# VectorE's attention order, 64x64 inverses on four array quarters, and an overwritten product ahead of each decay and rate product

## The reference, cut to what matters

```
def rwkv_step(S, inp):
    r_t, w_t, k_t, v_t, kk_t, b_t = inp
    sa = jnp.einsum('bhvk,bhk->bhv', S, -kk_t)
    S = S * w_t[:, :, None, :] + sa[..., None] * b_t[:, :, None, :] + v_t[..., None] * k_t[:, :, None, :]
    return S, jnp.einsum('bhvk,bhk->bhv', S, r_t)
```

## Time and profile before

| | us |
|---|---|
| median of 3 runs (4037.75 to 4045.4) | 4042.69 |
| the profiled execution | 4034.62 |
| its span, first to last instruction | 4032.9 |
| TensorE busy | 3566.0 |
| VectorE busy | 1768.2 |
| ScalarE busy | 1299.9 |

### The profile page before, as it was taken

One profiled execution on the slowest core, in us unless ns is written; L12 is line 12 of the kernel. 1 busy time (PEld: TensorE's weight loads), 2 busy tenths in 40 slices (PEclk: granted clock), 3 DMA queues, 4 the chain that ended last, 5 costly groups with the idle time before them and its releaser, 6 DMA issues. The chain is left out here.

```text
span 4032.9 us, 84425 instructions
## 1 busy us (share of the span) xinstructions
PE 3566.0 (88%) x32662; PEld 3292.9 (82%) x32662; DVE 1768.2 (44%) x2693; ACT 1299.9 (32%) x2505; POOL 161.6 (4%) x188
## 2 busy tenths in 40 slices
PE   6988689978888999999889985998698889999996
PEld 6988467768878999999878873777588789999996
DVE  3254445534654343333443534555345543333344
ACT  3343344414452111111333434443235521111113
POOL 0010000001000000000200000000001000000002
PEclk9999789979999999999989987989799899999998
DMA  2122220107541111111121123001176211111111
GB/s 93 53 68 68 69 62 26 68 25 262 210 140 32 42 43 50 42 48 46 46 70 51 62 70 100 21 26 73 61 256 220 95 37 47 47 42 46 47 47 54
DMA packets 240704, 298.79 MB, mean 74 GB/s; under 512 B 26616, under 2 KB 195952, under 8 KB 239504
## 3 DMA queue, kind: packets, MB, share of 16 engines
q1 hardware_dynamic: 224368, 227.83, 17.8%
q0 software_dynamic: 16032, 66.75, 4.3%
HBM read 228.91 MB, written 65.63 MB: 73 GB/s over the span
## 5 line engine op out<-in xcount | busy, mean ns | idle before, releaser
L767 PE MATMUL PS<-HH,WH 128*128 128x352 f32 (+2 forms) x3584 | 1194.4, 333 | 86.1 <-PEq L751 85.4
L767 PE MATMUL PS<-HH,WL 128*128 128x352 f32 (+2 forms) x3584 | 1167.6, 326 | 0.0
L767 PE MATMUL PS<-HL,WH 128*128 128x352 f32 (+2 forms) x3584 | 1166.4, 325 | 0.0
L767 PEld LDWEIGHTS PS<-HH,WH 128*128 128x128 f32 x3584 | 687.4, 192 | 104.8 <-issue 100.8
L767 PEld LDWEIGHTS PS<-HH,WL 128*128 128x128 f32 x3584 | 687.8, 192 | 2.8 <-issue 0.3
L767 PEld LDWEIGHTS PS<-HL,WH 128*128 128x128 f32 x3584 | 685.4, 191 | 0.0
L2307 DVE TENSOR_TENSOR WL<-WRAW,WH 128x1024 fp32r<-128x1024 f32 x192 | 243.6, 1269 | 680.2 <-DVEq L2306 680.2
L1517 ACT CAST WH<-WRAW 128x1024 fp32r<-128x1024 f32 x216 | 226.3, 1048 | 632.8 <-ACTq L1526 585.1
L1487 PE MATMUL PS<-GH,WH 128*128 128x352 f32 x1056 | 340.1, 322 | 0.0
L1487 PE MATMUL PS<-GH,WL 128*128 128x352 f32 x1056 | 339.5, 322 | 0.0
L1487 PE MATMUL PS<-GL,WH 128*128 128x352 f32 x1056 | 339.5, 322 | 0.0
(11 more groups left out here) (324 smaller groups left out, 4879.9 us busy)
## 6 DMA issues: line engine op xcount, KB each, us to landing
WRAW<-in_w_gate_up SPq DMA_DIRECT2D x88, 512.0 KB, 3.7
W<-split_dram SPq DMA_DIRECT2D x48, 512.0 KB, 4.6
WRAW<-in_w_down SPq DMA_DIRECT2D x44, 512.0 KB, 3.4
WH<-split_dram SPq DMA_DIRECT2D x40, 512.0 KB, 3.8
WL<-split_dram SPq DMA_DIRECT2D x40, 512.0 KB, 4.7
WRAW<-in_w_in SPq DMA_DIRECT2D x38, 512.0 KB, 3.8
raw_dram<-MIX SPq DMA_DIRECT2D x24, 528.0 KB, 3.1
R<-raw_dram SPq DMA_DIRECT2D x24, 512.0 KB, 4.5
```

The lines of the kernel that those rows point to most:

```text
L767: ins = e.matmul(out, lhs(k, wp), rhs(k, xp), start=first, stop=(k == n - 1 and xp == 1))
```

## The change

Four things change. In VectorE's attention `tile`, `normalised(1)` moves ahead of `rotary`, and the `lo` of the first two of the four due groups moves ahead of the masks. In the inverse, the blocks of head 1 are kept on the rows of the other chunk, so that the four blocks of a tile use all four 64x64 quarters of the array; each head has its own PSUM bank, both products of a level share one semaphore, and TensorE waits once in the middle of `level_right`. To put one operand there, `by_token` replaces one of its four transposes by a half one and two 64x64 products. Ahead of each decay or rate product of 512 columns, for the pairs after the first, a full 128-row product with the identity writes the same PSUM bank; the real product then overwrites it.

```diff
@@ constants: masks 128 wide, the attention masks in another order ...
-    C_AE = C_LV + LEVELS * 2 * CHUNK
+    C_AE = C_LV + LEVELS * 2 * P
...
+    def inverse_rows(h, c):
+        return slice((c ^ h) * CHUNK, (c ^ h) * CHUNK + CHUNK)
+    def column_of(u, x, h, part=0):
+        return (left_bank(u) + h) * 512 + part * 256 + x * CHUNK
+    def by_head(x, tiles):
+        return x[:, 0:2 * tiles, :].rearrange("p (a h y) t -> p h a (y t)", h=2, y=2)
+    def half_banks(u, part, tiles):
+        at = left_bank(u) * 512
+        return PS[:, at:at + 1024].rearrange("p (h z) -> p h z", h=2)[:, :, part * 256:part * 256 + tiles * HEAD]
@@ TensorE, by_token
-                transposes([... for o, a in enumerate((BB, KF, VV, KK))], 6 + x % 2, "chain_for_scalar", take)
+                for o, a in enumerate((BB, KF, VV)):
+                    e.matmul(PS[:, at + o * P:at + (o + 1) * P], rows_of(j, a)[:, tok:tok + P], ident, is_transpose=True, start=True, stop=True)
+                e.matmul(PS[:, at:at + HEAD], kk[0:HEAD, tok:tok + P], CST[0:HEAD, C_I64:C_I64 + HEAD], is_transpose=True, start=True, stop=True)
+                for c in range(2):
+                    ins = e.matmul(PS[inverse_rows(1, c), at + HEAD:at + P], kk[HEAD:P, tok + c * CHUNK:tok + (c + 1) * CHUNK],
+                                   CST[HEAD:P, C_I64:C_I64 + HEAD], start=True, stop=True)
@@ TensorE, level_left
-                    returned(a)
-                        ins = e.matmul(PS[r, at:at + CHUNK], masked_part(j, 0, u)[r, g, :], XX[u][r, g, :], start=True, stop=True)
+                    returned(a, b)
+                        ins = e.matmul(PS[inverse_rows(h, c), at:at + CHUNK], masked_part(j, 0, u)[r, g, :], XX[u][r, g, :], start=True, stop=True)
@@ TensorE, level_right
-                            ins = e.matmul(PS[r, at:at + CHUNK], XT[u][r, g, :], T1[u][r, g, :], start=True, stop=True)
-                        ins.then_inc(S("chain_for_vector"), 1)
-                        ins = e.matmul(PS[r, at:at + CHUNK], T1[u][r, g, :], XT[u][r, g, :], start=True, stop=True)
+                            e.matmul(PS[r, at:at + CHUNK], XT[u][i, g, :], T1[u][i, g, :], start=True, stop=True)
+                    for head in range(2):
+                        for x, h, g, c, r, p in blocks(tiles):
+                            if h == head:
+                                ins = e.matmul(PS[i, at:at + CHUNK], T1[u][i, g, :], XT[u][i, g, :], start=True, stop=True)
+                                if (x, h, c) == (0, 0, 0) and s < LEVELS - 1:
+                                    ins.then_inc(S("pe_done"), 1)
+                        if head == 0 and s < LEVELS - 1:
+                            e.wait_ge(S("pe_done"), 1)
+                            e.sem_inc(S("pe_done"), -1)
@@ TensorE, prepare, numbers 0 to 5
+                        if j > 0 and z - a == 512:
+                            e.matmul(out, ident, TWA[:, a:z], start=True, stop=True)
                         e.matmul(out, LW[p, 0:P], TWA[p, a:z], start=True, stop=True).then_inc(S("z_out"), 1)
@@ VectorE, attention tile
                 normalised(0, P, 256)
+                normalised(1, P, 256)
                 rotary(i * P, P, i % 2)
-                normalised(1, P, 256)
+                raw_lows(range(d[0] - 1, d[1]))
                 masked(0, P, 256, mask)
                 masked(1, P, 256, mask)
-                raw_lows(range(d[0] - 1, d[3]))
+                raw_lows(range(d[1], d[3]))
@@ VectorE, first_inverse: three copy_predicated of half the blocks (128, 64 and 64 rows) for one
@@ VectorE, level: one wait, then XX and XT out of both banks
-                            wait_for("chain_for_vector")
-                            e.copy_predicated(x[:, 0:n, :], ...).then_inc(S(f"bank{b}"), 1)
+                    wait_for("chain_for_vector")
+                            ins = e.copy_predicated(by_head(x, tiles), ..., half_banks(u, k, tiles).rearrange("p h (a z) -> p h a z", z=P))
+                    ins.then_inc(S(f"bank{left_bank(u)}"), 1)
```

More of the change, by code:

```diff
@@ L63 @@
 C_LV = C_TWO + CHUNK
-C_AE = C_LV + LEVELS * 2 * CHUNK
-C_AO = C_AE + 2 * 256
-C_EPS = C_AO + 256
+C_AE = C_LV + LEVELS * 2 * P
+C_AO, C_AF = C_AE + P, C_AE + 2 * P
+C_EPS = C_AE + 4 * P
 C_COLS = C_EPS + 2
@@ L1045, in solved @@
                 for u, tiles in units(j):
-                    returned(right_bank(u))
+                    returned(left_bank(u), right_bank(u))
                     b0 = 4 - 4 * u
-                    for half in range(tiles // 2):
-                        take(b0 + half)
-                        for x, h, g, c, r, p in blocks(tiles):
-                            if x // 2 == half:
-                                at = (b0 + half) * 512 + (x % 2 * 2 + h) * P
-                                ins = e.matmul(PS[r, at:at + P].rearrange("p (a t) -> p a t", a=2), XT[u][r, g, :],
-                                               TOK[u][r, x, 3:5, h * HEAD:(h + 1) * HEAD], start=True, stop=True)
-                        ins.then_inc(S("chain_for_scalar"), 1)
+                    take(b0, b0 + 1)
+                    for x, h, g, c, r, p in blocks(tiles):
+                        at, i = (b0 + h) * 512 + x * P, inverse_rows(h, c)
+                        ins = e.matmul(PS[r, at:at + P].rearrange("p (a t) -> p a t", a=2), XT[u][i, g, :],
+                                       TOK[u][i, x, 3:5, h * HEAD:(h + 1) * HEAD], start=True, stop=True)
+                    ins.then_inc(S("chain_for_scalar"), 1)
             def transitions(j):
                 for u, tiles in units(j):
-                    for half in range(tiles // 2):
-                        returned(4 - 4 * u + half)
+                    returned(4 - 4 * u, 5 - 4 * u)
                     b0 = 2 - 2 * u
@@ L1759, in level @@
                     from_psum("chain_for_scalar")
-                    a = left_bank(u)
-                    copy(T1[u][:, 0:2 * tiles, :], bank(a, 0, tiles * P).rearrange("p (g t) -> p g t", t=CHUNK)).then_inc(S(f"bank{a}"), 1)
+                    copy(by_head(T1[u], tiles), half_banks(u, 0, tiles).rearrange("p h (a z) -> p h a z", z=P)).then_inc(S(f"bank{left_bank(u)}"), 1)
             def solved(j):
                 for u, tiles in units(j):
-                    for half in range(tiles // 2):
-                        b = 4 - 4 * u + half
-                        from_psum("chain_for_scalar")
-                        e.activation(PQ[u][:, half * 4:half * 4 + 4, :], bank(b).rearrange("p (y t) -> p y t", t=P), ACT.Copy, scale=-1.0).then_inc(S(f"bank{b}"), 1)
+                    from_psum("chain_for_scalar")
+                    for h in range(2):
+                        b = 4 - 4 * u + h
+                        ins = e.activation(PQ[u][:, h:2 * tiles:2, :], bank(b, 0, tiles * P).rearrange("p (y t) -> p y t", t=P), ACT.Copy, scale=-1.0)
+                    ins.then_inc(S(f"bank{4 - 4 * u}"), 1)
             def state_out(j):
```

81 lines of the change are left out of this document (38 added, 43 removed).

## The result

The changed kernel takes 4061.87 us (median of 11 runs, 4045.73 to 4081.07), the kernel before 4042.69 (11 runs beside them). The ratio is 1.0059, with a 95% interval of 1.0040 to 1.0077: slower by 0.6%, where 0.8% faster was forecast. The profiled execution of the changed kernel took 4061.7 us, with a span of 4059.9, 27 more than before's. From here on, lines of the changed kernel that moved have its own numbers: L758 is now L771 (in `by_token` L989 to L993), L767 is L780, L999/L1031/L1036 are L1020/L1046/L1051, L1175 is L1192.

What follows compares the result with a forecast made beforehand. TensorE was taken as the bound, busy 3566 of 4033 us. Attention 36 and inverse 12 won, `by_token` 9, overwritten products 10 and constants 1 lost: 28 us, forecast 4010, 8-in-10 range 3972 to 4043.

Steps and rivals of the forecast that it cites:

- by_token: First parts of pairs: each call costs 0.15 us more, 0.3 at the lower clock; 9 us lost, bounds 2 and 16.
- The inverse: Inverses on four quarters: shorter TensorE groups, limited by VectorE and clock; net 12 us won, bounds 27 lost and 45 won.
- chain of levels: Inverse: hand-worked end of each level on VectorE; pairs 1 and 2 gain 4 us each, 25 us in two layers.
- The attention: Attention: VectorE's new order removes TensorE waits and half-speed time; 36 us won, bounds 20 and 43.
- by_key: Attention: TensorE's waits for probabilities in eight passes a layer shrink; at most 7 us won.
- The overwritten products: First parts: 24 added products are paid but give back clock; 10 us lost, bounds 33 lost and 3 won.
- first_inverse: Start of the inverse, pair 0: VectorE's three operations for one take 0.8 us longer, so pair 0 gains only 1.8.
- the half clock: Inverses: TensorE's new waits bring half-speed stretches, up to 27 us in eight pairs, half of it taken.
- So a group of 32 falls from 0.93 to 0.5 us: Inverse: groups using four quarters run at 16 ns a product; 11 us of TensorE a pair, 88 in eight pairs.
- the loop: Pair 3's inverse: one level through both units takes 5.4 us against 5.6, gaining 3.6 in all.
- the clock falls in the inverses: Rival, chance 0.12: half-speed clock in inverses makes the kernel slower, near 4060 at 2 us a pair, 4095 at 6.

Runs made afterwards that it cites:

- pace: The kernel before, plus two closing stretches of 2048 64x64 product instructions on TensorE, waiting for no other engine: 62.5 us on four quarters, 60.5 on two.

## Why the prediction was wrong

Two steps failed. The inverse was to win 12 us net and won nothing: its chain of levels was right, but the rate of 16 ns a product was taken to last, and waits for instructions had no term. And what the inverse needs ahead of it was put at 9 us and cost about 43, 26 for `by_token` and 17 for VectorE's copies.

- **The attention** was right: 36 forecast, 34 and 26 measured. The two sums of long waits went, 20.5 us. Half-speed time in the two attentions fell by 7 us each, worth 7 where 9 was taken. Only `by_key` gave 2.8 us instead of 7.
- **The overwritten products** were right in size, 10 forecast and 7 measured alone, for the reason given: they pay 27 us and take 48 us of half-speed time away, worth 24. In the whole change they may cost more, 17 by the medians.
- **`by_token`** is a term mis-sized. It was put at 0.15 us in 52 dense calls and a few us for the clock, 9 in all, bounds 2 and 16. Taking it out gives 26. The 16 calls of pair 0 were put at nothing, since TensorE waits in that part; they cost 0.58 us each where they run at the half clock, and 10.6 us in the two parts. The other 52 cost some 0.2 us each, and in the profiles the clock stays low longer (216 us of half-speed time against 113), which one execution of each does not settle.
- **VectorE's `first_inverse`** is the step that had no price of its own where it fell. The 0.8 us were put on pair 0 alone, inside the inverse. The 0.8 us hold for one unit; in a pair the copies take 1.4 us more, and they stand ahead of the operation that frees a bank for `centred`, which TensorE reaches first: 17 us by the run without them. What was missing is the question who waits for the instruction *behind* the longer one.
- **The inverse**: "So a group of 32 falls from 0.93 to 0.5 us" is the step that failed. It holds within a block (813.86 to 814.37 for L1046, with both row halves writing one bank), but it was read from 122 products, which with their weight loads are 244 instructions, fewer than a block of 256. The chain behind it was right: where neither stall nor half clock falls into an inverse, pair 2 gains the forecast 4 us. In pair 3 the loop was put at 5.4 us; from the group at 809.85 to the next such group at 817.12 it is 7.27 us with the two `variances` products of 1.98, so 5.3, and the level before, from 802.91 to 809.85, takes 6.94 with a stall of 1.43, so 5.5 and the stall. By the fit the chain gives 30 us where 25 were forecast; in after the stalls, which had no term, take 19 back and the half clock 18 where 13 were taken, together more than the gain.
- **The rival "the clock falls in the inverses"** gave a time, 4060, near the one that came, and its sign was seen: 17 us at half speed became 62, worth some 18 us. That its time was met is luck: it has the overwritten products at their full 33 us and `by_token` at 9, and the change lost its time in the first parts.

The Trainium skill (Runtime: NRT & Kernel Launch, Instruction fetch mechanics) says that a long program is streamed in blocks of 16 KiB, 256 instructions, and that crossing one is mostly hidden. The size agrees with the rows of the instruction queue; that it is hidden holds in `pace` for the two-quarter products at 29 ns, which show no stall, and not for those at 16 ns, where a crossing in the rows shown costs 1.4 to 1.9 us.

By single parts the sum is 34 and 26 (mean 30) won, 7 and 42 lost: 19 slower. Measured is 24 by the ratio, 19 by the medians.

## What to carry to other kernels

When an edit speeds up one engine's inner group, price its helpers as carefully as the group: here the quarters' gain went into waits for instructions and into time at the half clock, and a slower transpose step and a longer VectorE step in front of them lost some 43 us. For a VectorE operation that becomes longer, look at the next one in its queue and at who waits for that. And where a group's instructions become very short, check whether they can be supplied, and do not take their rate from a stretch shorter than a block: before already had 9 waits with no releaser, 7 of them in `transitions`, whose products took 16 ns, and the list of DMA queues has a row for the instructions.

## What the runs showed of the hardware

- TensorE's instructions arrive in transfers of 16 KB for 256 instructions; in `pace`, where nothing else was waited for, 3.5 to 4.0 us lay between two blocks, which is 27 to 31 ns for a product with its weight load. Products of 64x64 on four quarters (16 ns) run at that speed only within a block.
- An f32 product counts as two instructions on TensorE, a transpose as one.
- The three conditional copies of 256 columns, one on 128 rows and two on 64, took 0.45 us each, the one on 128 rows by 512 columns 0.67: half the rows saved nothing, half the columns a third.
- An overwritten product of 128 rows by 512 columns (1.05 us) can be free: four of them in pair 0's first part, where TensorE waits anyway, took the half-speed time there from 24 us to 10 in layer 0 and cost the stage nothing (31.7 and 31.8 us). The part did not become shorter either, so where the 0.27% of the whole run would come from is not shown.
